# The first two feed-forward tiles by ordinary products, and the low parts of weight slots in four GpSimd instructions of 128 columns

## What is computed

```python
x = x + gate1 * (mixed @ w_out[l])
h = rms_norm(x, norm2_g[l]) * (1.0 + scale2) + shift2
x = x + gate2 * conv_ffn(h, ffn_w_gate[l], ffn_w_up[l], ffn_conv_w[l], ffn_w_down[l])

def conv_ffn(h, w_gate, w_up, conv_w, w_down):
    a = causal_depthwise_conv(h @ w_gate, conv_w)      # three taps along the tokens
    return (jax.nn.gelu(a) * (h @ w_up)) @ w_down       # hidden width 2816
```

## Time and profile before

| | us |
|---|---|
| median of three runs | 1900.75 |
| the profiled execution | 1902.17 |
| its span, first to last instruction | 1900.3 |
| PE busy in the span | 1829.5 |
| DVE busy | 1143.4 |
| POOL busy | 858.5 |
| ACT busy | 587.4 |

### The profile page before, as it was taken

The page is one execution under the profiler, slowest core; times in us unless marked ns, Lnnn a source line. Parts: engine busy times, 40 slices in busy tenths (PEclk is TensorE's granted clock), DMA queues, the critical chain, the costliest instruction groups (busy, mean ns, idle before and its releaser), DMA issues.

```text
span 1900.3 us, 34410 instructions
## 1 busy us (share of the span) xinstructions
PE 1829.5 (96%) x14002; PEld 1458.5 (77%) x14002; DVE 1143.4 (60%) x1698; ACT 587.4 (31%) x947; POOL 858.5 (45%) x978
## 2 busy tenths in 40 slices
PE   6999999999999999999999999779999999999996
PEld 4788777767887887887788787558888888888884
DVE  3856578754545555545444835866566565665656
ACT  4341344452213213213122413432223332233233
POOL 2767556523322232232232845545545445455443
PEclk9999999999999999999999999789999999999998
DMA  8616211232122132131134541021111201111022
GB/s 331 217 45 232 100 56 67 79 130 82 40 96 79 40 97 78 36 101 57 58 106 168 174 164 34 0 67 38 52 66 44 66 24 64 66 44 58 30 67 89
DMA packets 72029, 163.55 MB, mean 86 GB/s; under 512 B 6112, under 2 KB 30816, under 8 KB 71904
## 3 DMA queue, kind: packets, MB, share of 16 engines
q1 hardware_dynamic: 64416, 142.88, 22.2%
q10 hardware_dynamic: 7488, 18.88, 2.7%
HBM read 133.17 MB, written 28.57 MB: 85 GB/s over the span
## 4 chain that ended last, share of the span: by engine, by line
PE 83%; DVE 9%; issue 3%; ACT 2%; POOL 2%; DMA 1%; SPq 0%; POOLq 0%; ACTq 0%; DVEq 0%
PE gbank L792 34%; PE gbank L1340 17%; PE mbank L1424 11%; PE mbank L1117 3%; PE mbank L1340 3%; PE gbank L1264 1%; PE gbank L827 1%; DVE state L2559 1%; DVE fa L2305 1%; POOL fa L744 1%; PE gbank L1117 1%; PE mbank L873 1%; PE mbank L1040 1%; PE gbank L894 1%; DVE fa L2232 1%
## 5 line engine op out<-in xcount | busy, mean ns | idle before, releaser
L625 POOL TENSOR_TENSOR w_hi<-w_raw,zero 128x256 fp32r<-128x256 f32 (+1 forms) x260 | 206.1, 823 | 621.2 <-PE gbank L792 601.0
L792 PE MATMUL gbank<-h_hi,w_hi 128*128 128x512 f32 x976 | 396.2, 406 | 0.5 <-POOL w_lo L629 0.5
L792 PE MATMUL gbank<-h_lo,w_hi 128*128 128x512 f32 x976 | 386.8, 396 | 0.0
L792 PE MATMUL gbank<-h_hi,w_lo 128*128 128x512 f32 x976 | 386.5, 396 | 0.0
L675 POOL TENSOR_TENSOR ra<-late,ra 128x256 fp32r<-128x256 f32 x204 | 184.5, 929 | 266.8 <-ACT ra L1888 266.7
L629 POOL TENSOR_TENSOR w_lo<-w_raw,w_hi 128x256 fp32r<-128x256 f32 (+1 forms) x260 | 252.8, 1003 | 5.1
L1340 PE MATMUL gbank<-h_hi,ra 128*128 128x512 f32 x704 | 229.1, 400 | 12.2 <-DVE h_lo L2705 8.7
L792 PEld LDWEIGHTS gbank<-h_hi,w_hi 128*128 128x128 f32 x976 | 183.3, 188 | 51.9 <-issue 14.5
L1424 PE MATMUL mbank<-ffn_a,ra 128*128 128x512 f32 x960 | 219.2, 389 | 0.0
L792 PEld LDWEIGHTS gbank<-h_hi,w_lo 128*128 128x128 f32 x976 | 183.2, 188 | 40.6 <-issue 1.5
L792 PEld LDWEIGHTS gbank<-h_lo,w_hi 128*128 128x128 f32 x976 | 183.5, 188 | 39.3 <-issue 2.9
(11 more groups left out here) (401 smaller groups left out, 2879.1 us busy)
## 6 DMA issues: line engine op xcount, KB each, us to landing
w_raw<-in_w_tail SPq DMA_DIRECT2D x72, 512.0 KB, 3.8
fa<-in_w_ada SPq DMA_DIRECT2D x48, 512.0 KB, 6.5
w_raw<-in_w_in SPq DMA_DIRECT2D x26, 512.0 KB, 4.3
p_scr<-fa ACTq DMA_DIRECT2D x20, 512.0 KB, 2.6
w_raw<-in_w_mix SPq DMA_DIRECT2D x16, 640.0 KB, 4.0
fa<-in_xT SPq DMA_DIRECT2D x16, 512.0 KB, 8.1
w_raw<-in_w_gate SPq DMA_DIRECT2D x16, 512.0 KB, 4.1
sig_scr<-fa ACTq DMA_DIRECT2D x32, 256.0 KB, 2.1
```

The source lines that it names most:

```text
L625: last = pool.tensor_tensor(hi[:, c], raw[:, c], zero[:, 0:1].to_broadcast([P, w]), ALU.add)
L792: mm = pe.matmul(gb[bank], w, r, start=(q == 0), stop=(q == 3 * ks - 1))
```

## The change

Tiles 0 and 1 are computed by ordinary products. PE runs `std_half(0)`, the first 512 tokens of both tiles over all eight channel blocks, and then `std_half(1)`, the second 512; these need all four quarters of h but none of the sums. The sums of h for the products 1, 4, 3, 6 and 7 are made on DVE during that time and after it; POOL makes none any more. The first 14 slots with ten weight sums become eight slots of plain weights. The gate of tiles 0 and 1 is copied out and convolved in halves of 512 tokens (`std_gate`, `std_conv2`, `std_conv3`, `std_gelu`, `std_mul`, `std_act_hi`, `std_act_lo`). Group 0 gets its own order: for tile 2 the products 2, 5, 4, 3, 1, then the down projection of tiles 0 and 1, then 6 and 7, then tile 3. From group 1 on the order is as before. Apart from this, `slot_lo` makes each low part in four instructions of 128 columns, in all slots of the feed-forward part.

```diff
-SLOTS_A, SLOTS_G = 14, 18
-SUMS_A, SUMS_G = 10, 10
+SLOTS_A, SLOTS_G = 8, 18
+SUMS_G = 10
...
-                for c in (slice(0, 256), slice(256, HALF)):
+                for c in (slice(n_ * P, n_ * P + P) for n_ in range(4)):
                     last = pool.tensor_tensor(lo[:, c], src[:, c], hi[:, c].bitcast(F32), ALU.subtract)
                 last.then_inc(sem("s_lo"), 1)
...
+            def std_part(t, hf, k):
+                for up in range(2):
+                    n = (k // 4) * 4 + 2 * t + up
+                    if hf == 0 and k % 4 == 0:
+                        pe.wait_ge(sem("s_lo"), n + 1)
+                    hi, lo = ring(n)
+                    c, cols = slice(k % 4 * P, (k % 4 + 1) * P), slice(hf * HALF, (hf + 1) * HALF)
+                    for which, (w, r) in enumerate(((hi, h_hi), (hi, h_lo), (lo, h_hi))):
+                        mm = pe.matmul(std_bank(t, up, hf), w[:, c], r[:, k, cols], start=k == 0 and which == 0, stop=k == KT - 1 and which == 2,
+                                       skip_group_check=True)
...
+            def std_half(hf):
+                nm = ("11", "21") if hf == 0 else ("12", "22")
+                for k in range(KT):
+                    label = "lo" + nm[k // 4]
+                    pe.wait_ge(sem(label), at(label, k % 4))
+                    for t in range(2):
+                        std_part(t, hf, k)
+                    if hf == 0 and k == 1:
+                        sum_over_channels(1)
...
-            for t in range(2):
-                pe.wait_ge(sem("s25"), t + 1)
-                first_product(6 + t)
...
+                    before = {2: ("act_mul", 1), 5: ("c12", 2), 4: ("r2", 1), 3: ("s25", 1), 1: ("c12", 6), 6: ("c12", 9), 7: ("c21", 1)}
+                    pe.wait_ge(sem(before[p_][0]), before[p_][1])
+                    product(p_, bank, n, n, p_ in (2, 5, 1), None if p_ in (2, 5) else f"lo{p_}")
...
-            ffn_tile(0, 0, 0, SLOTS_A)
-            ffn_down(0, 0)
+            second_tile(2, 5, 4, 3, 1)
+            ffn_down(0, 0, 5)
+            second_tile(6, 7)
             ffn_tile(0, 0, 1, SLOTS_A + 11)
...
+            act.wait_ge(sem("e7"), at("e7", 3))
+            std_act_hi(0, 0)
+            std_act_hi(1, 0)
+            tile_slot(0, 0, 0, THEN.index(1))
+            std_gate(0, 1)
+            std_gate(1, 1)
+            std_gelu(0, 1)
+            act.wait_ge(sem("lo3"), at("lo3", 3))
+            r2(SLOTS_A + 1, 0, Q[0])
+            std_gelu(1, 1)
```

More of the change, by code:

```diff
@@ L397, in h_terms @@
             return h_hi[:, k, c], h_lo[:, k, c]
-        FIRST = [(p_, t_) for p_ in (2, 4, 5, 3, 6, 1, 7) for t_ in range(2)]
-        FIRST_SUMS = [x_ for x_ in FIRST if x_[0] not in (3, 4)]
         THEN = (2, 5, 4, 3, 1, 7, 6)
         THEN_SUMS = (2, 5, 1, 7, 6)
+        GROUP0 = (2, 5, 4, 3, 1, "down", "down", "down", "down", 6, 7)
         def terms(prod, up, gate):
@@ new lines, in c12, with c21, r2 @@
+            def c12(made, odd):
+                act.wait_ge(sem("prod"), made)
+                act.activation(G[:, UP], banks(odd)[0], ACT.Copy).then_inc(sem("c12"), 1)
+            def c21(made, odd):
+                act.wait_ge(sem("prod"), made)
+                act.activation(U[:, LO], banks(odd)[1], ACT.Copy).then_inc(sem("c21"), 1)
+            def r2(made, odd, into):
+                act.wait_ge(sem("prod"), made)
+                act.activation(into, banks(odd)[1], ACT.Copy).then_inc(sem("r2"), 1)
@@ new lines, in _ @@
+            std_gate(0, 1)
[4 more added lines that the diff above has]
+            std_gelu(1, 1)
+            std_act_hi(0, 1)
+            down_slot(0, 0, 0, 5)
+            std_act_hi(1, 1)
+            down_slot(0, 0, 1, 5)
+            c12(SLOTS_A + 4, 0)
+            down_slot(0, 0, 2, 5)
+            down_slot(0, 0, 3, 5)
+            act.wait_ge(sem("act_lo"), 4)
+            c21(SLOTS_A + 3, 0)
@@ L2878, in _ @@
-            tile_sum(0, 0, 0, 0)
-            tile_sum(0, 0, 0, 1)
-            q_of(0, 11, Q[0], 0)
-            c22(0, 9, Q[0], 0)
+            std_mul(1, 0)
+            for j in range(4):
+                lo3(j)
+            for j in range(4):
+                e6(j)
+            for j in range(4):
+                e7(j)
+            dve.wait_ge(sem("lo3"), at("lo3", 3))
             tile_sum(0, 0, 0, 2)
+            std_act_lo(0, 0)
+            std_act_lo(1, 0)
             tile_sum(0, 0, 0, 3)
-            q_of(1, 12, Q[1], 1)
@@ L2901, in _ @@
-            dve.tensor_copy(cwc[:, 3:6], par[:, cw0 + 3:cw0 + 6]).then_inc(sem("small_set"), 1)
-            dve.wait_ge(sem("small_set"), 6)
-            conv1(1, kept(1))
-            conv2(1, kept(1))
-            conv3(1, kept(1))
-            def down_add(i, off, m):
-                n0 = i * SLOTS_G + (off * SLOTS_G + SLOTS_A + 7)
+            tile_sum(0, 0, 0, 4)
+            for t in range(2):
+                std_conv2(t, 1)
+                std_conv3(t, 1)
+            std_mul(0, 1)
+            s25(2, SLOTS_A + 2, Q[0], 0)
@@ L2910, in down_add @@
+            std_mul(1, 1)
+            std_act_lo(0, 1)
+            std_act_lo(1, 1)
+            def down_add(i, off, m, base=7):
+                n0 = i * SLOTS_G + (off * SLOTS_G + SLOTS_A + base)
                 if m % 2:
@@ L2962, in group @@
                 conv3(t1, kept(1))
-            group(0, 0)
+            for j in range(4):
+                lo6(j)
+            q_of(2, SLOTS_A + 5, Q[0], 0, gb[2])
+            down_add(0, 0, 0, 5)
+            lo7(0)
+            down_add(0, 0, 1, 5)
+            lo7(1)
+            lo7(2)
+            down_add(0, 0, 2, 5)
+            lo7(3)
+            down_add(0, 0, 3, 5)
+            dve.tensor_copy(cwc[:], par[:, cw0 + 6:cw0 + 12]).then_inc(sem("small_set"), 1)
+            tile_sum(0, 0, 1, 0)
+            tile_sum(0, 0, 1, 1)
+            down_add(0, 0, 4, 5)
+            down_add(0, 0, 5, 5)
+            tile_sum(0, 0, 1, 2)
+            down_add(0, 0, 6, 5)
+            down_add(0, 0, 7, 5)
+            c22(2, SLOTS_A + 10, Q[0], 0)
+            c11(2, SLOTS_A + 11, Q[0], 0)
+            dve.wait_ge(sem("small_set"), 6)
+            conv1(2, kept(0))
+            conv2(2, kept(0))
+            conv3(2, kept(0))
+            tile_sum(0, 0, 1, 3)
+            tile_sum(0, 0, 1, 4)
+            s25(3, SLOTS_A + 13, Q[0], 1)
+            mul(2)
+            tile_sum(0, 1, 0, 0)
+            tile_sum(0, 1, 0, 1)
+            act_lo(2, 0)
+            tile_sum(0, 1, 0, 2)
+            tile_sum(0, 1, 0, 3)
+            q_of(3, SLOTS_A + 16, Q[0], 1)
+            c11(3, SLOTS_A + 17, Q[0], 1)
+            conv1(3, kept(1))
+            conv2(3, kept(1))
+            c22(3, SLOTS_A + 18, Q[0], 1)
+            conv3(3, kept(1))
             with dve.Fori(0, NG - 2) as i:
```

587 lines of the change are left out of this document (281 added, 306 removed), and 10 rows, old and new, of the table NORM2.

## The result

The forecast was 1874.6 us, 1864 to 1885, and faster.

What follows compares the result with a forecast made beforehand. PE's matmul count was taken to bound the loop, DVE feeding PE the seam before it. Against the profiled 1902.17 us, - 40.7 + 5.4 + 6.1 + 2.5 + 0.5 gave 1876.0, so a median of 1874.6 us, range 1864 to 1885.

Steps and rivals of the forecast that it cites:

- What bounds the kernel: From 1279 to 1858 us PE's matmul count; from 1180 to 1279 us DVE feeding PE too slowly, 40.7 us lost.
- The ordinary products run without a gap: Both halves of tiles 0 and 1 on PE without waits: 44.7 us, from 1179.84 to 1224.5.
- The walk of DVE's list: DVE's instructions beside and after the ordinary products, 0.87 us a step beside POOL; `e7` ends at 1229.5 (1226.0 to 1231.4).
- e6: Four DVE instructions before the four `e7`, beside POOL's pieces for tile 2's slots; 0.87 us each (0.62 to 1.01).
- The new wait: At tile 2's product 4, PE waits for ACT's copy `r2`, queued behind a wait for `e7`: 6.1 us (2.0 to 8.3).
- The clock behind it: Matmuls slowed by the low clock after PE's wait at tile 2's product 4: 2.5 us (1.5 to 3.0).
- `c21`: In tile 3, ready at 13.7 us while product 7 needs it at 13.6; charged 0.5 us (0 to 2.5).
- The sum: Against the profiled 1902.17 us: - 40.7 + 5.4 + 6.1 + 2.5 + 0.5 = - 26.2, so 1876.0.
- POOL's extra load in a round: In the loop, four pieces instead of two add 4.5 us to POOL's 29.8 of a 59.9 us round, costing nothing.
- the cover holds throughout: Rival at tile 2: product 4 finds `r2` ready and the clock stays up; gain 35.3, 1865.5 us; chance 0.20.
- The second stall: Rival: product 3, the down projection or tile 3 waits, another 3 to 5 us plus clock; 1879 to 1885; chance 0.17.
- The loop on POOL: Rival: POOL's pieces bound the loop once a slot exceeds 3.3 us; 1965, or near 1920 at 3.6; chance 0.04.

Runs made afterwards that it cites:

- run 1: Changed kernel with the ordinary products for tiles 0 and 1 only, each low part again in two POOL instructions of 256 columns: 1877.14 us, 0.9876 of the kernel before.
- run 9: Changed kernel with every feed-forward low part in eight instructions of 64 columns, in the loop too: 1883.65 us, 0.9910 of the kernel before.
- the second trace: The unaltered changed kernel, timed and traced once more beside the first experiments: 1874.77 us, 0.9864 of the kernel before.
- run 4: Changed kernel plus 22 matmuls with unused result on PE between tile 2's products 5 and 4, filling the idle time: 1874.92 us, 0.9860 of the kernel before.
- run 3: Changed kernel with ACT's copy `r2` ahead of its wait for `e7` and DVE's sum `s25` ahead of `act_lo`: 1870.74 us, 0.9840 of the kernel before.
- run 7: Changed kernel with `r2` early and DVE's weight sums, `s25`, convolution and ACT's gate copies also moved forward: 1870.06 us, 0.9836 of the kernel before.
- run 5: Changed kernel with the low parts of the first 19 blocks in eight instructions of 64 columns, the loop unaltered: 1873.29 us, 0.9858 of the kernel before.

## Why the prediction was right, step by step

- *What bounds the kernel.* Right: the loop is 519.35 to 519.41 us in the kernel before and in nearly every one above, 519.59 in run 1, with POOL's round anywhere from 29 to 39 us. Only run 9 moved it.
- *The ordinary products run without a gap.* Right: 1180.68 to 1225.11, 44.43 us against 44.7. The sum of squares, which I let cost 1.15, cost PE about 0.9.
- *The walk of DVE's list.* Counted from the seam's start, the second half's scaling began at 8.24 us (8.6 forecast) and `e7` ended at 48.7 (49.7). The step of `e6` and `e7` beside pieces of 128 is 0.87 us, the value worked out from the steps beside 256 and 512. The Trainium skill (SBUF — State Buffer, section Who interferes with whom) has the second of two such instructions, a DVE one with two SBUF inputs and a GpSimd one that reads SBUF, blocked until the first is done: 0.60 + 0.43, the piece alone (1.72 for four), would be 1.03. The measured 0.87 is less, and 0.73 beside pieces of 64 is less than 0.60 + 0.28 (sixteen alone took 4.53 in run 9), so the traces show less than full exclusion.
- *The new wait.* The right place and releaser, 5.4 us where I had 6.1 (5.6 in the second trace). The path to it is the one forecast, through DVE's convolution: done 54.2 us behind the seam's start, forecast 55.0. Two slips beside it did no harm. The "five steps" of ACT are seven, since each copy of `std_gate` is two instructions; they end near 1233.2, before the gelu may start. And the cover of 13.6 us for the down projection's first blocks is five products, while 4, 3 and 1 are 8.16; it was enough, since in run 4, where they ran at full clock, no wait stands in front of the down projection.
- *The clock behind it.* 3.1 us where I had 2.5; 2.0 in the second trace (36 matmuls in 10.20). Run 4 shows that this is the price of standing still: with the wait filled they took 8.45.
- *`c21`.* 0.2 us where I had 0.5.
- *The sum.* From the seam's start I had 26.2 us, and the traces have 26.17 and 26.9. The two sizes that were off, the wait (0.7 too long) and the clock (0.6 too short), lay on opposite sides and cancel; that the first trace meets the sum to 0.03 us is luck.
- *Mis-sized without effect.* POOL's extra load in a round is 8.0 us, not 4.5. Four pieces alone take 1.72 us where I had 1.65, which makes 5.8 for 18 slots; the rest I put down to pieces beside DVE, which is not measured apart.
- *Not foreseen.* I carried the profiled execution's time over as if everything outside the seam stayed. In the first trace 0.84 and 1.88 us came back there, in the second the start was 2.4 us earlier than before. That scatter is as large as the terms that I argued about.
- *The rivals.* That the cover holds throughout would have needed `r2` ahead of the wait for `e7`; run 3 shows that even then the down projection waits. The second stall did not come. The loop on POOL is not near at 128.

## What to carry to other kernels

Where one engine feeds another with operands, count how many matmuls each operand serves: with 24 matmuls more, 5.4 us, the seam is 23 to 25 us shorter, and each block of the list covers four times the work (what the shorter list in front of it adds is not separated). In an in-order queue look for what stands behind a wait that it doesn't need: moving one copy past it, with the sum that the next product needs, was worth 4 us. Finer pieces on a contending engine shift the delay from one engine to the other, and they pay as long as the one that gets it has cover; read that cover where the load is thickest, not from a mean.

## What was not expected of the hardware

The two traces of the changed kernel differ by 4.8 us in span: 3.25 in front of the seam, 0.72 in it and 0.83 behind the loop. In front of it there are two places. One is near the start. Windows of the two traces (columns as in the earlier trace rows), first the one with the later seam:

```profile
30.00:35.00 5.00, 3.00 (x46) 1.99 (x37) 4.75 (x5) 2.30 (x2) 0.00 (x0) 0.89 1.05 389
35.00:40.00 5.00, 5.00 (x20) 4.05 (x19) 3.53 (x5) 1.87 (x2) 0.00 (x0) 0.77 1.05 387
```

then the other:

```profile
30.00:35.00 5.00, 3.56 (x57) 2.56 (x58) 4.00 (x5) 2.30 (x2) 0.00 (x0) 1.00 1.05 387
35.00:40.00 5.00, 5.00 (x51) 4.00 (x54) 4.87 (x6) 2.31 (x2) 0.00 (x0) 1.00 1.05 387
```

The second is near 417 us, in the same order:

```profile
415.00:420.00 5.00, 4.17 (x17) 2.81 (x14) 1.43 (x10) 2.78 (x6) 0.00 (x0) 0.66 0.15 38
```

```profile
415.00:420.00 5.00, 5.00 (x25) 4.00 (x23) 2.69 (x17) 3.03 (x7) 0.00 (x0) 1.00 0.57 160
```

At the same places in the program the clock falls in one and not in the other, and the seam starts at 1180.68 or 1177.43. The other traces go with that: run 7 has neither fall and starts at 1178.09, run 5 only the second (0.66) and 1179.45, run 4 both (0.65 and 0.74) and 1181.33. A further place is the final down projection, behind a wait of 2.67 us that all have, here in the first trace and in the second:

```profile
1839.60 4.56 PE L1436 MATMUL mbank<-ffn_a,ra 128*128 128x512 f32 x12 [2.67 <-DVE ffn_a L2842]
```

```profile
1835.63 3.02 PE L1436 MATMUL mbank<-ffn_a,ra 128*128 128x512 f32 x12 [2.67 <-DVE ffn_a L2842]
```

The same 12 matmuls behind the same wait take 4.56 or 3.02 us; the second trace loses part of that again further on, so that the whole of what is behind the loop differs by 0.83. Which of the two an execution gets is not explained by anything here; nobody should read it as an effect of a change.
